# Mixed attention of a three-part model's first two layers: probabilities left unnormalized, outputs formed token by token, scaled when copied out, turned at the end

## The reference

```python
# three attention branches, 8 heads of 64 each
o_a = g_cmp * cmp + g_sel * selected + g_win * window     # three softmax attentions, each times a gate per token and head
o_b = softmax over a band of 128 keys, with a sink logit in the denominator
o_c = causal softmax attention on latents (queries and keys 96 wide, values 64 wide)
p = softmax(where(mask, scores, -1e30)); o = p @ v
merged = g_a * (o_a @ w_branch_a) + g_b * (o_b @ w_branch_b) + g_c * (o_c @ w_branch_c)
x = x + merged @ w_out                                     # then the feed forward part and a gated projection
```

## Time and profile before

| | |
|---|---|
| three runs | 3032.72, 3031.27, 3031.72 us |
| span of the profiled execution, first to last instruction | 3030.8 us |
| TensorE busy in the span | 2586.0 us |
| VectorE, ScalarE busy | 2113.4, 1087.8 us |
| mean granted clock of TensorE, share of full speed | 0.942 |

### The profile page before, as it was taken

The page is one execution under the profiler, slowest core; times in us unless marked ns, Lnnn a source line. Parts: engine busy times, 40 slices in busy tenths (PEclk is TensorE's granted clock), DMA queues, the critical chain, the costliest instruction groups (busy, mean ns, idle before and its releaser), DMA issues. The chain is left out here.

```text
span 3030.8 us, 35565 instructions
## 1 busy us (share of the span) xinstructions
PE 2586.0 (85%) x13090; PEld 1885.0 (62%) x13090; DVE 2113.4 (70%) x4116; ACT 1087.8 (36%) x1979; POOL 607.0 (20%) x573
## 2 busy tenths in 40 slices
PE   8999999999999899899887666678999887666766
PEld 7968997896899797797543222226888653222222
DVE  6467665657765565555898888866674699888876
ACT  4365444436444465444221111113644222112111
POOL 0000000000000000001445444440000254444442
PEclk9999999999999999999998888889999998988888
DMA  6423554441455433254999999997434899999997
GB/s 255 172 100 126 183 183 152 180 174 70 157 181 187 152 140 113 96 181 160 418 427 421 427 426 426 427 427 295 165 112 146 343 418 423 426 426 427 426 426 306
DMA packets 112493, 810.80 MB, mean 268 GB/s; under 512 B 12736, under 2 KB 12736, under 8 KB 14272
## 3 DMA queue, kind: packets, MB, share of 16 engines
q0 software_dynamic: 73728, 536.90, 42.2%
q1 hardware_dynamic: 38592, 271.63, 24.5%
HBM read 807.44 MB, written 1.05 MB: 267 GB/s over the span
## 5 line engine op out<-in xcount | busy, mean ns | idle before, releaser
L3511 PE MATMUL ps<-arena 128*128 128x512 f32 x912 | 522.2, 724 | 239.1 <-ACT arena L3407 239.0
L167 DVE TENSOR_TENSOR ring_low<-ring,parts 128x2048 fp32r<-128x2048 f32 x214 | 488.0, 2291 | 310.6 <-ACT parts L161 306.8
L480 PE MATMUL ps<-parts,parts 128*128 128x256 f32 x2528 | 569.7, 283 | 2.5 <-PEq L393 1.7
L3511 PEld LDWEIGHTS ps<-arena 128*128 128x128 f32 x912 | 201.9, 231 | 547.0 <-ACT arena L3407 321.0
L480 PE MATMUL ps<-parts,ring_low 128*128 128x256 f32 x1824 | 511.9, 281 | 0.0
L161 ACT ACTIVATE parts<-ring 128x2048 fp32r<-128x2048 f32 x214 | 406.8, 1913 | 274.6 <-PE ps L488 105.7
L488 PE MATMUL ps<-parts,parts 128*128 128x512 f32 x1344 | 439.0, 396 | 5.8 <-DVE ring_low L167 3.8
L480 PEld LDWEIGHTS ps<-parts,parts 128*128 128x128 f32 x2528 | 428.1, 189 | 3.7 <-issue 2.1
L3234 POOL DMA_INDIRECT arena<-in_experts,stage_index x276 | 323.0, 1170 | 531.7 <-PE ps L3511 224.2
L3511 PE MATMUL ps<-ring,arena 128*128 128x512 f32 x616 | 316.0, 650 | 106.5 <-ACT arena L3407 106.2
L3282 DVE CUSTOM_DVE_ANT_0 arena<-arena 128x1024 f32<-128x1024 f32 x276 | 333.6, 1227 | 96.9 <-DMA arena<-in_experts,stage_index 94.0
(11 more groups left out here) (504 smaller groups left out, 2968.0 us busy)
## 6 DMA issues: line engine op xcount, KB each, us to landing
ring<-in_stream SPq DMA_DIRECT2D x249, 1024.0 KB, 4.8
arena<-in_experts,stage_index POOLq DMA_INDIRECT x276, 22.9
ring<-in_experts,stage_index POOLq DMA_INDIRECT x236, 24.6
gain_row<-in_gain_rows SPq DMA_DIRECT2D x4, 512.0 KB, 5.7
arena<-in_mem SPq DMA_DIRECT2D x2, 1024.0 KB, 4.8
arena<-in_stream SPq DMA_DIRECT2D x2, 1024.0 KB, 8.2
par<-in_params SPq DMA_DIRECT2D x4, 386.0 KB, 4.4
x<-in_x SPq DMA_DIRECT2D x1, 1024.0 KB, 4.8
```

The costliest lines, as they stand in the source:

```text
L167: dve.tensor_tensor(k.ring_low[v % SLOTS], whole, self.high_of(v).bitcast(F32), ALU.subtract).then_inc(self.ph.sem("chunk_split"), 1)
L480: last = pe.matmul(self.ps[:, 2 * pair + f // 2, (f % 2) * T:(f % 2 + 1) * T], w[:, f * P:(f + 1) * P], x[:, k, :], start=(k == 0 and i == ...
L3511: last = pe.matmul(k.ps[:, bank + n, :], diag[:, s % ROWS, :], rows[row_of[s]][:, D + n * BLK:D + (n + 1) * BLK], start=(s % SLOTS_PER_TOK ...
```

## The change

Probabilities stay unnormalized, and the scale step of VectorE is gone. The values carry a 65th column of ones (set by GpSimd), so that each output has the sum of its row as a last column. In `values` the turned probabilities (128 columns) become the stationary operand and the values (65 columns) the moving one, and the output is token-major: 4 x 65 columns on 128 partitions. `turn` waits for the exponentials alone, whose accumulation is dropped. `out` takes the reciprocal of the sum from PSUM and multiplies on the way to SBUF; where the output is added, it is four instructions, one for each head, and semaphore waits of VectorE on itself. The outputs are turned to feature-major at the end: those of branches a and b by four `turn_outs` of four transposes in steps 16 to 19 of the attention (through PSUM bank 7, from which ScalarE and VectorE make the high and low parts, in halves), those of branch c by eight transposes after the first block of `back_phase`.

```diff
@@ -891,8 +891,8 @@
-        self.branch_high, _ = k.at_parts(a, CHUNK)
-        self.values, a = k.at(a, MT, 8, HD)
+        self.branch_high, _ = k.at_parts(a + MT * 8, CHUNK)
+        self.values, a = k.at(a, MT, 8, HD + 1)
@@ -900,10 +900,9 @@
-        self.vcmp, a = k.at(a, 2, HD)
-        self.vC, a = k.at(a, MT, 8, HD)
+        self.vC, a = k.at(a, MT, 8, HD + 1)
-        self.oT, a = k.at(a, 3, 4, T)
+        self.o, a = k.at(a, 3, 2, MT, T)
@@ -1009,6 +1009,9 @@
+                pool.wait_ge(ph.sem("windows_padded"), 2)
+                pool.memset(z.values[:, :, :, HD:HD + 1], 1.0).then_inc(ph.sem("ones_column"), 1)
+                pool.wait_ge(ph.sem("ones_column"), 1)
@@ -1075,7 +1078,7 @@
-                link(act.activation(z.values, values, ACT.Copy))
+                link(act.activation(z.values[:, :, :, 0:HD], values, ACT.Copy))
@@ -1137,7 +1140,13 @@
         def out_ps(b):
-            return k.ps[:, 6, 0:T]
+            return k.ps[:, 6, 0:4 * (HD + 1)].rearrange("p (h e) -> p h e", h=4)
+
+        def added_before(b):
+            return sum(1 for bt in batches[:b] if bt.add)
+
+        def sinks_before(b):
+            return sum(1 for bt in batches[:b] if bt.sink is not None)
@@ -1156,6 +1165,10 @@
+                pool.memset(z.vcmp[:, :, HD:HD + 1], 1.0).then_inc(ph.sem("ones_columns"), 1)
+                pool.wait_ge(ph.sem("ones_columns"), 1)
+                pool.memset(z.vC[:, :, :, HD:HD + 1], 1.0).then_inc(ph.sem("ones_columns"), 1)
+                pool.wait_ge(ph.sem("ones_columns"), 2)
@@ -1191,7 +1204,7 @@
-                    pe.wait_ge(ph.sem("probs_scaled"), b + 1)
+                    pe.wait_ge(ph.sem("probs_exp"), 4 * (b + 1))
@@ -1206,13 +1219,12 @@
-                    for pair in ((0, 2), (1, 3)):
-                        for i in range(len(bt.key_tiles)):
-                            for h in pair:
-                                v, n = bt.value(h, i), bt.key_tiles[i][1]
-                                base, at = HD * (h // 2), h % 2
-                                last = pe.matmul(out_ps(b)[base:base + HD, at * P:(at + 1) * P], v, probsT[0:n, b % 2, i, h, :],
-                                                 start=(i == 0), stop=(i == len(bt.key_tiles) - 1))
+                    if b == 12:
+                        pe.wait_ge(ph.sem("ones_columns"), 2)
+                    for h in range(4):
+                        for i, (_, n) in enumerate(bt.key_tiles):
+                            last = pe.matmul(out_ps(b)[:, h, :], probsT[0:n, b % 2, i, h, :], bt.value(h, i),
+                                             start=(i == 0), stop=(i == len(bt.key_tiles) - 1))
@@ -1292,6 +1304,17 @@
+
+                def turn_outs(i, pair):
+                    pe.wait_ge(ph.sem("out_copied"), 9 + 3 * pair) if i == 1 else pe.wait_ge(ph.sem("out_added"), 4 * (7 + pair))
+                    if i == 1 and pair == 0:
+                        pe.wait_ge(ph.sem("c_copied"), 8)
+                    else:
+                        pe.wait_ge(ph.sem("heads_split"), 2 * (1 - i) + pair)
+                    for f in range(2):
+                        for m in range(MT):
+                            last = pe.transpose(spare[:, f * T + m * P:f * T + (m + 1) * P], z.o[:, i, pair, m, f * P:(f + 1) * P], k.ident[:])
+                    last.then_inc(ph.sem("outs_turned"), 1)
@@ -1324,6 +1347,8 @@
+                    if b >= 16:
+                        turn_outs((1, 1, 0, 0)[b - 16], b % 2)
@@ -1360,28 +1385,32 @@
-                def scale(b):
-                    bt = batches[b]
-                    dve.wait_ge(ph.sem("probs_exp"), b + 1)
-                    s = sums[:, b, :]
-                    if bt.sink is not None:
-                        link(dve.tensor_tensor(s, s, nmax[:, b, :], ALU.add))
-                    link(dve.reciprocal(s, s))
-                    if bt.coef is not None:
-                        link(dve.tensor_tensor(bt.per_group(s), bt.per_group(s), bt.coef, ALU.mult))
-                    p = probs[:, b % 3, :, 0:bt.n_keys]
-                    dve.tensor_tensor(p, p, bc(s.unsqueeze(2), [P, 4, bt.n_keys]), ALU.mult).then_inc(ph.sem("probs_scaled"), 1)
-
-                    o = out_ps(b).rearrange("p (h n) -> p h n", h=2)
+                    o, total, s = out_ps(b)[:, :, 0:HD], out_ps(b)[:, :, HD], sums[:, b, :]
+                    if bt.sink is None:
+                        link(dve.reciprocal(s, total))
+                    else:
+                        dve.wait_ge(ph.sem("sinks_exp"), sinks_before(b) + 1)
+                        link(dve.tensor_tensor(s, total, nmax[:, b, :], ALU.add))
+                        link(dve.reciprocal(s, s))
+                    if bt.coef is not None:
+                        link(dve.tensor_tensor(bt.per_group(s), bt.per_group(s), bt.coef, ALU.mult))
                     if bt.add:
+                        if added_before(b) > 0:
+                            dve.wait_ge(ph.sem("out_added"), 4 * added_before(b))
-                        ins = dve.tensor_tensor(bt.out, o, bt.out, ALU.add)
+                        for h in (0, 2, 1, 3):
+                            part = bt.out[:, h % 2, h // 2, :]
+                            ins = dve.scalar_tensor_tensor(out=part, in0=o[:, h, :], scalar=s[:, h:h + 1], in1=part, op0=ALU.mult, op1=ALU.add)
+                            ins.then_inc(ph.sem("out_added"), 1)
+                        dve.wait_ge(ph.sem("out_added"), 4 * added_before(b) + 4)
+                        dve.sem_inc(ph.sem("out_copied"), 1)
-                        ins = dve.tensor_copy(bt.out, o)
-                    ins.then_inc(ph.sem("out_copied"), 1)
+                        dve.tensor_tensor(bt.out, o.rearrange("p (g l) e -> p l g e", g=2),
+                                          bc(s.rearrange("p (g l) -> p l g", g=2).unsqueeze(3), [P, 2, 2, HD]), ALU.mult
+                                          ).then_inc(ph.sem("out_copied"), 1)
@@ -1415,10 +1444,11 @@
-                def heads_low(i, turn):
-                    dve.wait_ge(ph.sem("heads_high"), turn)
-                    dve.tensor_tensor(z.oT_low[:, i], z.oT[:, i], z.heads_high[:, i].bitcast(F32), ALU.subtract
-                                      ).then_inc(ph.sem("heads_split"), 1)
+                def heads_low(i, pair):
+                    dve.wait_ge(ph.sem("heads_high"), 2 * (1 - i) + pair + 1)
+                    tiles = slice(2 * pair, 2 * pair + 2)
+                    dve.tensor_tensor(z.oT_low[:, i, tiles], spare.rearrange("p (a t) -> p a t", a=2), z.heads_high[:, i, tiles].bitcast(F32),
+                                      ALU.subtract).then_inc(ph.sem("heads_split"), 1)
@@ -1429,13 +1459,12 @@
                 for b in range(nb):
-                    scale(b)
-                    if b == 19:
-                        heads_low(1, 1)
+                    if b >= 17:
+                        heads_low(*((1, 0), (1, 1), (0, 0))[b - 17])
@@ -1454,7 +1483,7 @@
-                heads_low(0, 2)
+                heads_low(0, 1)
@@ -1466,11 +1495,10 @@
-                        link.note(act.activation(p, p, ACT.Exp, bias=nmax[:, b, h:h + 1], accum_out=sums[:, b, h:h + 1]))
-                    link.sync()
+                        act.activation(p, p, ACT.Exp, bias=nmax[:, b, h:h + 1]).then_inc(ph.sem("probs_exp"), 1)
                     if bt.sink is not None:
-                        link(act.activation(nmax[:, b, :], k.stat[:, 7, 4 * (b % 16):4 * (b % 16) + 4], ACT.Exp))
-                    act.sem_inc(ph.sem("probs_exp"), 1)
+                        act.wait_ge(ph.sem("probs_exp"), 4 * (b + 1))
+                        act.activation(nmax[:, b, :], k.stat[:, 7, 4 * (b % 16):4 * (b % 16) + 4], ACT.Exp).then_inc(ph.sem("sinks_exp"), 1)
@@ -1509,9 +1537,10 @@
-                def heads_high(i, outs):
-                    act.wait_ge(ph.sem("out_copied"), outs)
-                    act.activation(z.heads_high[:, i], z.oT[:, i], ACT.Copy).then_inc(ph.sem("heads_high"), 1)
+                def heads_high(i, pair):
+                    act.wait_ge(ph.sem("outs_turned"), 2 * (1 - i) + pair + 1)
+                    act.activation(z.heads_high[:, i, 2 * pair:2 * pair + 2], spare.rearrange("p (a t) -> p a t", a=2), ACT.Copy
+                                   ).then_inc(ph.sem("heads_high"), 1)
@@ -1603,10 +1631,17 @@
+                def turn_outs(pe):
+                    for pair in range(2):
+                        for f in range(2):
+                            for m in range(MT):
+                                last = pe.transpose(k.ps[:, 4 + pair, f * T + m * P:f * T + (m + 1) * P], z.o[:, 2, pair, m, f * P:(f + 1) * P], k.ident[:])
+                    last.then_inc(ph.sem("outs_turned"), 1)
+
-                    k.linear_T(pe, ph, lin, (z.heads_high[:, i], z.oT_low[:, i]), split)
+                    k.linear_T(pe, ph, lin, (z.heads_high[:, i], z.oT_low[:, i]), split, between={(0, 1): turn_outs} if i == 0 else {})
@@ -1636,7 +1671,8 @@
```

(20 more changed lines are left out.)

## The result

The changed kernel takes 3050.8 us (median of four runs, 3048.83 to 3059.88) against 3031.49: a ratio of 1.0070, 95% interval 1.0056 to 1.0084, which is 17 to 25 us more. The medians are 19.3 us apart. The slowest run had a mean granted clock of 0.936, the other three 0.940 to 0.943. The span of the profiled execution is 3050.3 us, 19.5 more than before.

A forecast was written before the change was run, and what follows sets the result against it. TensorE's own queue was taken as the bound, with 10.1 us of waits a layer to give back. Terms 10.5 + 2.1 + 1.0 + 1.5 + 0.2 - 10.1 = +5.2 us a layer, +10.4 on 3031.7: 3042 us, range 3033 to 3051.

The forecast's parts named there:

- The scale step goes: Attention: TensorE's waits for a busy VectorE vanish, if no wait comes in their place; -10.1 us a layer.
- The product: Attention's values product turned round: 224 passes at 0.113 us, 25.3 us against 14.8 before; +10.5 us a layer.
- The upper end, 0.128: Values product: highest price considered, 0.128 us a pass, that of 128 moving columns in a transpose; 6.5 us more, 3048.6.
- rival 3: Values product: loads overlap, 0.069 us a pass, 15.5 us a layer; kernel faster, 3025.5 us; chance 11%.
- Turning the outputs: Added TensorE transposes: four groups of four in the attention, +2.1 us; eight for branch c in the back phase, +1.0.
- new waits: Attention, mostly from step 16 on: waits in the tight closing chain and copying before it; +1.5 us a layer, between 0 and 4.
- last out: End of the attention: a reciprocal and a multiplication in place of a copy of 0.42 us; +0.2 us a layer.
- Rival 2: Values groups: changing tiling mode drains TensorE, so neighbours get cheaper, 2.6 us a layer; about 3036 us; chance 17%.
- Costed at nothing: ... the place of the values: Where the widened values stand in memory was taken to cost no time.
- Rival 1: Attention: one more 6.9 us half-clock stretch in each layer, costing 3.4 us each; 3049 us; chance 15%.
- the prediction's own signs of being wrong: One-tile values well under 0.8 us, waits of several us in steps 16 to 19, or clock falling where it was full.

The follow-up runs named there:

- e4: Kernel before without the scale step (no sink, reciprocal, gate or multiplication), transposes waiting for the exponentials, output unnormalized: 3016.92 us, ratio 0.9953.
- e3: Kernel before with the values product alone turned round; scale step kept, no column of ones, no turning of outputs: 3044.32 us, ratio 1.0039.
- e7: e1 with the third and fourth turning of outputs put into free score banks, so they wait for no low part: 3047.53 us, ratio 1.0058.
- e2: Kernel before with only operand places in SBUF moved to where the change has them: 3036.91 us, ratio 1.0017.
- e1: Changed kernel with unused words putting the normed input's parts and the heads' low part at old places or 256 bytes beside: 3044.76 us, ratio 1.0041.
- e10: Kernel before with everything behind the latents' values 384 bytes lower, the normed input at its old place: ratio 1.0011.
- e6: e1 with five idle TensorE products, one ahead of the last values product and four behind it: 3046.33 us, ratio 1.0049.

## Why the prediction was right and wrong

The direction and the prices of the parts hold: the attentions, the transposes and the waits come to 9.8 us where the forecast had 10.4. What the sum left at nothing is as large again. By its steps:

- *The scale step goes, -10.1.* Right in the changed kernel: none of the waits for it is left. e4 shows that this isn't so by itself: without the longer product, ScalarE's exponentials would have come up behind it and only 5.75 us a layer would have been gained.
- *The product, +10.5.* Right: 10.7, by 0.108 to 0.118 us a pass against the 0.113 taken from the small products of the project phase, and 10.9 in e3. The upper end, 0.128, and rival 3 with its 0.069 fell. The advice of the Trainium skill ("TensorEngine Tiling (Array Packing)", When to Use Tiling), to make the narrow operand stationary and pack two of them, held: 15.1 us against 25.8. The Trainium skill's columns over 1.2 GHz ("TensorE: Matmul & The Clock Gate", LDWEIGHTS) give an estimate of 107 ns for a load of 128 columns, just under the lower edge of what was measured for a pass, 108 ns.
- *Turning the outputs, +2.1 and +1.0; new waits, +1.5; last out, +0.2.* The outputs cost 2.1 and 0.9, the last out 0.2, as forecast. The new waits are 2.7 at full clock, 1.2 more than forecast though within its 0 to 4, and they stand elsewhere: 1.3 are for the additions, which I had thought covered by 1.6 us of other work. They are 0.86 us for four and with reciprocal, gate and VectorE's waits for itself some 1.3. The wait for the bank of the turned outputs is 0.4, and e7 gave 0.6 us a layer.
- *Rival 2, drains of switching.* Something of it may be there: TensorE's other groups got 1.7 us a layer cheaper, 0.8 of it in the transposes ahead of the product (0.09 us for a two-tile batch). Not the 2.6 us a layer, and no run shows that it is the switching. The forecast had nothing for this. That the attention came out at 4.0 us against its 4.2 is therefore in part luck: these 1.7 us make up for the waits.
- *"Costed at nothing: ... the place of the values."* **This is the step that failed.** It costs 3.0 us in the triples of the profiled execution and some 5 by the medians (e2: 5.2, 2.4 to 7.9 by the interval; e1 gives back some 6 and brings the kernel within reach of the forecast). I looked at the widened tiles for what they contain, not for what they push along. The price comes in products that the change doesn't touch.
- *Rival 1, the clock, 15%.* It came in part, and a term for the clock is missing from the sum: the second step that failed. The forecast left layer 2's one stretch of half clock as it was. Layer 1's attention had one of 6.8 us after the change, worth 2.4 us (98.27 against 95.86) where the rival had 3.4, and one of 3.4 us opened each back phase, worth some 1.4 each; against that, two stretches of the kernel before are gone, of which the one in layer 2's attention was worth 1.7. The largest part, 3.7 us, stands in a later phase that neither the forecast nor the rival looked at. A granted clock that falls where it was full was among the prediction's own signs of being wrong.

Put together for the two profiled executions: 8.0 us in the attentions at full clock and 1.8 for branch c's transposes are the forecast's own terms. The places add 3.0. The clock adds 0.7 in the attentions (2.4 less 1.7), 2.8 in the openings of the back phases and 3.7 in the later phase, 7.2 in all. This makes 20.0 of 19.5 us. How much of the clock's part belongs to the change and how much to the one execution that was profiled is open.

The medians differ by 19.3 us, which is 1.9 times the forecast's 10.4 and leaves the changed kernel's 3050.8 just inside the range; by the ratio, 1.0070, it is 21 us, twice the forecast and just beyond the range's upper end of 3051.

## What to carry to other kernels

Look at what bounds the list of the engine that is given the work: waits are not free room for any work. TensorE had 11.0 us of them in 91.85, and 10.9 us of work in the values product (e3) filled only 3.5. A product whose narrow operand was stationary and packed cost 1.7 times as much turned round (15.1 and 25.8 us). When a tile is widened, keep the places of everything behind it (pad to the old distances), and compare the time of products that the change doesn't touch, and the granted clock of phases that it doesn't touch. Work that is shared out to relieve an engine must be looked for as waits on the engine that takes it.

## What was not expected of the hardware

- The place of operands in SBUF changes a pass of an fp32r product of 256 columns by up to 2% (0.353 to 0.360 us for three), with no instruction changed (e2): 80.67 and 81.73 us for one stretch of 674 passes. Shifts of the input's parts by 64 and 128 bytes cost, one by 256 bytes (e1) didn't, and one and the same shift of the later places cost in one layer and not in the other (e10). The rule is open.
- A multiplication of 128 x 768 in VectorE took 1.42 us with GpSimd at work on another head, and 0.96 us beside ScalarE.
- TensorE ran at half clock for 13.7 us with no gap in its list (e1, e6), more often with the turned product. A phase that the change doesn't touch had 12.0 us of half clock before and 19.8 after, and took 3.7 us longer.
